# Eight rows of a split activation, moved from a pitch of 2048 bytes to one of 2064

## The reference

```python
# first block
h = rms_norm(x, attn_norm)
proj = h @ w_in                                   # 1024 x ~7800 columns, split into 14 parts
o_a = dsa_attention(...)    # 4 heads, top-64 keys chosen by an indexer, bucket bias
o_b = hgrn2_mixer(...)      # gated linear recurrence, chunks of 64
o_c = mla_attention(...)    # latent attention with rope
x = x + (g_a * (o_a @ w_up_a) + g_b * (o_b @ w_up_b) + g_c * (o_c @ w_up_c)) @ w_out
h = rms_norm(x, ffn_norm)
x = x + (silu(h @ w_gate) * (h @ w_up)) @ w_down  # width 2816
x = rms_norm(x, final_norm)
# second block
x = x + 0.5 * swiglu(rms_norm(x, ffn1_norm), ...) # width 2816
h = rms_norm(x, mix_norm)
... h @ w_in_2, forgetting attention and stick-breaking attention, 8 heads each ...
x = x + (sigmoid(g_fox) * (y_fox @ w_fox) + sigmoid(g_sb) * (y_sb @ w_sb)) @ w_out
x = x + 0.5 * swiglu(rms_norm(x, ffn2_norm), ...) # width 2816
x = x + sigmoid(rms_norm(x, ple_norm) @ w_ple_gate) * (p @ w_ple_proj)
```

## Time and profile before

| | |
|---|---|
| median of three runs | 1059.9 us (1058.3 to 1060.31) |
| span of the profiled execution | 1057.7 us |
| its own time beside the span | not recorded apart; the runs lie 0.6 to 2.6 us above the span |
| TensorE matmul | busy 1047.9 us, 99% of the span, 8760 matmuls |
| TensorE weight load | busy 1020.3 us, 8760 loads |
| VectorE | 741.0 us, 70% |
| ScalarE | 579.6 us, 55% |
| GpSimd | 77.0 us, 7% |
| DMA | 187.81 MB, mean 178 GB/s |
| granted TensorE clock | 1.000 (2.4 GHz) |

### The profile page before, as it was taken

The page is one execution under the profiler, slowest core; times in us unless marked ns, Lnnn a source line. Parts: engine busy times, 40 slices in busy tenths (PEclk is TensorE's granted clock), DMA queues, the critical chain, the costliest instruction groups (busy, mean ns, idle before and its releaser), DMA issues.

```text
span 1057.7 us, 22212 instructions
## 1 busy us (share of the span) xinstructions
PE 1047.9 (99%) x8760; PEld 1020.3 (96%) x8760; DVE 741.0 (70%) x1098; ACT 579.6 (55%) x880; POOL 77.0 (7%) x92
## 2 busy tenths in 40 slices
PE   9999999999999999999999999999999999999998
PEld 8899999999999999999999999898889999999998
DVE  6799988747876666657666677667986876665666
ACT  5456655576565544556544445455666664554553
POOL 0000000001310000111000001041001300000110
PEclk9999999999999999999999999999999999999999
DMA  6356433344556554555555456464335455554563
GB/s 235 129 173 217 162 123 120 120 160 170 190 181 217 190 186 146 198 204 190 205 196 194 148 193 217 173 207 162 137 120 199 171 191 196 198 203 146 195 222 120
DMA packets 32444, 187.81 MB, mean 178 GB/s; under 512 B 3832, under 2 KB 7552, under 8 KB 14720
## 3 DMA queue, kind: packets, MB, share of 16 engines
q1 hardware_dynamic: 31472, 185.58, 50.3%
q0 software_dynamic: 416, 1.06, 0.4%
q10 hardware_dynamic: 496, 0.33, 0.2%
HBM read 184.98 MB, written 1.06 MB: 176 GB/s over the span
## 4 chain that ended last, share of the span: by engine, by line
PE 87%; DVE 6%; ACT 1%; issue 1%; DVEq 0%; ACTq 0%
PE acc L681 83%; PE area_a L681 2%; PE area_t L681 2%; DVE wlo L1575 2%; DVE s_sum L2133 0%; ACT he L1179 0%; ACT whi L1179 0%; PE area_t L947 0%; ACT s_a L1179 0%; DVE mask L1780 0%; DVE st L1765 0%; DVE score L1805 0%; DVE s_z L2135 0%; DVE s_a L2131 0%; DVE s_z L2037 0%
## 5 line engine op out<-in xcount | busy, mean ns | idle before, releaser
L681 PE MATMUL acc<-hs,whi 128*128 128x256 f32 x3584 | 624.6, 279 | 2.9 <-DVE wlo L1575 2.7
L681 PEld LDWEIGHTS acc<-hs,whi 128*128 128x128 f32 x3584 | 541.9, 187 | 10.1 <-issue 7.1
L681 PE MATMUL acc<-hs,wlo 128*128 128x256 f32 x1792 | 496.8, 277 | 0.0
L1179 ACT ACTIVATE whi<-raw 128x1024 fp32r<-128x1024 f32 (+3 forms) x379 | 357.2, 978 | 162.8 <-PE acc L681 136.6
L1575 DVE TENSOR_TENSOR wlo<-raw,whi 128x1024 fp32r<-128x1024 f32 (+4 forms) x259 | 272.1, 1092 | 98.5 <-ACT whi L1179 97.4
L681 PEld LDWEIGHTS acc<-hs,wlo 128*128 128x128 f32 x1792 | 336.1, 188 | 0.2
L681 PE MATMUL acc<-hid,whi 128*128 128x256 f32 x1056 | 180.9, 277 | 0.2 <-DVE wlo L1575 0.2
L681 PEld LDWEIGHTS acc<-hid,whi 128*128 128x128 f32 x1056 | 159.2, 188 | 0.4 <-DVE wlo L1575 0.4
L681 PE MATMUL acc<-hid,wlo 128*128 128x256 f32 x528 | 146.0, 277 | 0.0
L1663 DVE TENSOR_TENSOR wlo<-raw,whi 128x1024 fp32r<-128x1024 f32 x120 | 141.2, 1219 | 4.3 <-ACT whi L1179 4.2
L1676 DVE TENSOR_TENSOR hbuf<-acc,sbuf 128x256 f32<-128x256 f32 x66 | 28.0, 425 | 115.4 <-PE acc L681 112.0
(11 more groups left out here) (316 smaller groups left out, 1029.2 us busy)
## 6 DMA issues: line engine op xcount, KB each, us to landing
raw<-in_w_gu SPq DMA_DIRECT2D x66, 1024.0 KB, 4.8
raw<-in_w_dn SPq DMA_DIRECT2D x48, 704.0 KB, 4.0
raw<-in_w_up SPq DMA_DIRECT2D x10, 1024.0 KB, 4.8
raw<-in_w_gates1b SPq DMA_DIRECT2D x8, 1024.0 KB, 4.7
raw<-in_w_out SPq DMA_DIRECT2D x8, 1024.0 KB, 4.8
raw<-in_w_qk SPq DMA_DIRECT2D x8, 1024.0 KB, 4.8
raw<-in_w_gates SPq DMA_DIRECT2D x8, 1024.0 KB, 4.8
raw<-in_w_projT_b SPq DMA_DIRECT2D x7, 1024.0 KB, 4.8
```

The costliest lines, as they stand in the source:

```text
L681: return nc.tensor.matmul(out, w, m, start=start, stop=stop, skip_group_check=True)
L1179: return nc.scalar.activation(out, in_, f, **kw)
```

## The change

`hs` is allocated with 516 words in a row in place of 512, and only the first 512 of each are used. Row k then starts 2064 k bytes behind the start of `hs`, that is 16 k bytes further modulo 128 than before. No instruction is added or taken away. What differs is the SBUF address in every instruction that reads or writes a row of `hs` other than the first.

```diff
 ARENA = 29024
+HS_ROW = 2 * T + 4
...
         hs_off = base + 4 * ARENA
-        assert hs_off + 4 * KD * 2 * T <= nc.sbuf_usable_end
-        hs = at("hs", (KD, 2 * T), hs_off, F32R)
+        assert hs_off + 4 * KD * HS_ROW <= nc.sbuf_usable_end
+        hs = at("hs", (KD, HS_ROW), hs_off, F32R)[:, :, 0:2 * T]
         sq = at("sq", (KD, T), hs_off)
```

## The result

The changed kernel takes 1074.8 us (1074.4 to 1075.47), the kernel before 1059.5 us over its four runs in the same session. The ratio is 1.0144, with a 95% interval of 1.013 to 1.0159: 15.3 us more. The forecast was 1065.7 us with a range to 1073.5 us. The direction was right, the size was two and a half times what I had worked out, and the time lies outside the range.

The account below looks back on a forecast made before the run. The prediction took TensorE's back-to-back matmuls to bound the kernel. Moving reads of hs gave +7.8 and -2.0, so +5.8 us on a 1057.7 us span; with 2.2 us carried to the median, 1065.7 us, range 1054.5 to 1073.5 us.

Parts of the forecast that it names:

- What bounds the kernel: Whole kernel: TensorE's matmuls are busy 1047.9 of 1057.7 us, so time per matmul goes into the total unshortened.
- The two paces and their counts: Matmuls with hs moving: about 3,600 at a narrow pace of 113.3 ns and 1,750 at a wide one of 117.8 ns.
- The first access, the moving reads,: TensorE's moving reads of hs: six shifted rows of eight change the matmul pace, +5.8 us in sum.
- the worst case: Matmuls with hs moving: all narrow-pace ones go to the wide pace, +4.5 ns on 3,600, +16.2 us.
- The forecast's own range: Kernel time if narrow-pace matmuls lose 1 to 4 ns each: 1062 to 1071 us.
- The wider range: Kernel time over the forecast and its rivals: 1054.5 to 1073.5 us.
- the signs: Gate/up loops: uneven 115 to 117 ns, about 690 matmuls in 80 us; down products and hs writes unchanged.
- everything at the wide pace: Last rival, matmuls reading hs: any start off the fixed phase costs the wide pace, +14.2 us, 1074.1 us; chance 0.08.
- the wide pace goes away: Rival, matmuls reading hs: varied phases break a lockstep with the weight reads, -6.9 us, 1053.0 us; chance 0.17.
- The page's rule: SBUF reads: lines are 16 bytes, so shifts by whole lines change nothing, sum zero; given less than half.
- The other two accesses: Weight loads from hs and ScalarE's and VectorE's writes of hs: taken as nothing, bounded by 0.9 and 0.6 us.

Follow-up runs that it names:

- e2: Against the kernel before: all rows of hs start 64 bytes later, pitch kept at 2048 bytes; 1080.17 us, ratio 1.0195.
- e9: Against the kernel before: every tensor, weights included, starts 64 bytes later, so distances between them stay the same; 1059.26 us, ratio 1.0005.
- e15: Against the kernel before: only row 7 of hs starts 16 bytes later, pitch kept at 2048 bytes; 1067.76 us, ratio 1.0081.
- e1: Against the kernel before: all eight rows of hs start 16 bytes later, pitch kept at 2048 bytes; 1080.65 us, ratio 1.0201.
- e10: Against the kernel before: all rows of hs start 32 bytes later, pitch kept at 2048 bytes; 1080.2 us, ratio 1.0196.
- e8: Against the kernel before: arena and hs start 64 bytes later while the weights stay, so hs, hid, ms and osplit move against them; 1093.18 us, ratio 1.0315.
- e4: Against the kernel before: rows of hs lie 2176 bytes apart in place of 2048; 1070.4 us, ratio 1.0103.
- e12: Against the kernel before: pitch of hs kept at 2048 bytes, but rows 4 to 7 lie 128 bytes further; 1071.12 us, ratio 1.011.

## Why the prediction was wrong, step by step

**What bounds the kernel** was right. The 15.4 us more of busy TensorE went into the time whole, and the other engines absorbed it.

**The two paces and their counts** were right: about 3,620 and 1,650 of the 5,292 distances under 130 ns are at 112 to 114 and at 116 to 120 ns, against my 3,600 and 1,750.

**The first access, the moving reads,** is the step that failed. That this access is where the change costs was right; whose matmuls pay and how much was wrong. I had the cost come from a row's own start, off a multiple of 64. The runs show in its place a cost of the distance to the weights modulo 256, paid by the stream: in e2 every start is a multiple of 64 and the pace is 119.2 ns, and in e9 every address moves and nothing is paid. I priced the matmuls at the narrow pace at +2.9 ns, on six rows of eight, and gave the wide ones -1.5 ns: +7.8 - 2.0 = +5.8 us. Measured, the pace in the loops went from 113.33 to 117.86 ns, +4.5 ns, on all eight rows. With 3,600 x 8/8 x 4.5 = 16.2 us, which stands in the prediction as the worst case, and nothing for the wide ones the forecast would have been 1076 us, 1.3 us above the result. Two assumptions made it small:

- *That only a shifted row pays.* Row 0 was not moved and pays 5.4 ns. e15 shows why: with one row of eight shifted by 16 bytes, the time rises by 8.4 us, not by an eighth of e1's 21.5 us. A matmul's pace depends on how the stream stood before it.
- *That w_fvl's moving weights give the price.* Those rows were the nearest and pointed the right way, but they alternate between phases 32 bytes apart under short interrupted runs, and their mean lies between the paces. At a pitch of 2064 the rows meet eight phases modulo 128; of the four that were tried as constants, 64 gives the two paces and 0, 80 and 96 are worse than the wide one (e2, e1, e10).

**The ranges.** The forecast's own range of 1062 to 1071 us is said to stand for 1 to 4 ns; by the sum as it is written these give 1060.6 to 1068.7 us. The wider range ended at 1073.5 us, short of the last rival's 1074.1 us, and the result of 1074.8 us lies just there. Of the signs, the distances that vary with the row, the unchanged down products and the unchanged writes came as forecast, but the mean of 117.86 ns is above the 115 to 117 and the count is 681, not 690.

**The rival "everything at the wide pace"** came nearest (1074.1 us, to which I gave 0.08). Its number was right by luck: a start off the fixed place costs nothing by itself, as e9 shows, in which every address moved.

**The rival "the wide pace goes away"** named the right partners, the moving read and the weight read, and the wrong effect of the change on them. I held against it that blocks with 8 stationary columns show both paces too and concluded that the weight read was hardly the partner. That inference was wrong: e8 and e9 show that it is. A block inherits its pace from the stream ahead of it, so the paces of a short block say little of its own operands.

**The page's rule.** The Trainium skill's note on 16-byte lines in SBUF — State Buffer gave no change. e1 moves every row by exactly one such line and costs 21.5 us, so for this stream the rule does not describe what is paid. The Trainium skill's page TensorE: Matmul & The Clock Gate says in "Part 2: What happens when you issue a matmul", in its step on the weight load, that loading the next weights doesn't steal SBUF read bandwidth from the running matmul. The pair e8 and e9 does not agree: 34 us depend on the distance between the two reads.

**The other two accesses** were rightly priced at nothing; the writers of hs kept their 493 and 480 ns.

What stays open is the mechanism: no run here shows why the distance counts or why its period is 256 bytes. Phases other than 0, 64, 80, 96 and their partners 128 further were not tried as constants, and why a change of phase by the weights' address repairs the stream, while the same change by the moving row's address (e4, e12) does harm, is not settled.

## What to carry to other kernels

Where TensorE is busy all the time, measure the distance from start to start of equal matmuls on equal tiles; two values on the same operands mean that the stream has more than one rhythm, and a layout can shift the share of each. Keep the moving rows at one distance from the weights modulo 256 bytes from row to row, time that distance, since the constant ones of e1, e2 and e10 were the slowest, and check it after any change of allocation ahead of them, since 64 bytes of padding in the wrong place cost 3% here. Price a disturbance of such a rhythm over the whole stream, not over the instructions that were moved.

## What the runs showed of the hardware that was not expected

- The pace of 128x256 fp32r matmuls at the full clock is 113.3 ns or 117.8 ns where the phase between moving row and weights is 64 or 192, by the phase and by the history of the stream, and 119.1 to 119.5 ns where that phase is 0, 80 or 96 modulo 128.
- The period is 256 bytes: a pitch of 2304 costs nothing, one of 2176 costs 11 us.
- With one phase of 192 for everything, a run can stay at either pace for a whole layer, and the time of the kernel varies by 9 us from run to run in place of about 1.
- 128 bytes of padding before and behind one weight tensor, together with slots a multiple of 256 bytes apart and hs 128 bytes further, take 0.5% off the kernel's time with no work added or taken away.
